# A Trainium2 kernel of a hybrid encoder: the first gate block of the attention branch moved to the end of the recurrence

## The chip, the cores and the metric

The kernel runs on one core of a Trainium2 chip. A core has TensorE (PE in the profile; its weight loads are PEld), VectorE (DVE), ScalarE (ACT), GpSimd (POOL) and SyncE (SP). Each takes its instructions in the order in which they are written, and they meet by semaphores alone. PE writes into eight PSUM banks (bank0 to bank7, each 128 x 512 fp32), from which VectorE and ScalarE read. The metric is the device time in microseconds of one execution of the whole program.

## The reference, cut to what matters

Two layers, each over x of 256 tokens x 2048 channels:

```python
for i in range(DEPTH):                       # 2
    proj = x @ w_in[i]
    y_a = s5_mixer(a_x, ...)                 # recurrence, gelu, then y * sigmoid(y @ w_glu + b_glu)
    y_a = y_a * silu(a_z)
    y_b = hyena_mixer(b_u, ...) * silu(b_z)  # short and long convolutions
    y_c = mla_mixer(c_q, c_kv, c_kr, ...) * silu(c_z)   # 8 heads of attention
    lifted = einsum('blnc,ncd->blnd', stack([y_a, y_b, y_c]), w_lift[i])
    gates = sigmoid(gate_logits)             # 3 x 2048 columns of proj
    mixed = sum(gates * lifted, axis=2) @ w_out[i]
    x = layer_norm(ALPHA * x + mixed + ple)
```

What the change moves is a piece of `gate_logits`: x times 512 columns of w_in, in the first of four column groups of the branch y_a. The code calls that stage "lifta", since the lifting of y_a goes with it; its 24 blocks are multiplied while the attention heads run, which is why the change is named after the attention branch.

## The kernel before

All weights lie in 184 blocks per layer, 128 x 2048 fp32 each, which SyncE streams in order into a ring of two blocks (four half slots). For most blocks ScalarE writes a rounded high part WH (`make_wh`, L380) and VectorE the rest WL = raw - WH (`make_wl`, L394; in the recurrence `make_wl_quarter`, L385), four quarters each. WH and WL hold one block: a quarter is written again when PE is done with it, and the slot of the ring is freed by the WL of its quarters. PE multiplies three products per tile: high x high, high x low, low x high.

A layer runs through the stages "ax" (8 blocks), "s5" (the recurrence, a loop of 8 turns with 8 blocks each), "glu" (4 blocks, not split, L1556), "mla" (queries, keys and values, 6 blocks, not split, L1556 and L1797, then the 8 heads), "lifta" within the heads, "hyc", "lift", "ple" and "out". Only the order of the code sets the order of the work. The table FILLS counts how often each bank is filled in each stage; the semaphores psum_full and psum_free of a bank count through the whole layer, so each wait is worked out from it.

At the end of the last turn of the recurrence PE multiplies `outputs` (L1724, L1729) into bank 7. VectorE adds (L834) and GpSimd sends the tile through y_scratch in HBM and back, and ScalarE makes the GELU of it (L1356), on which the gated unit waits. Before it PE multiplies the sums of squares of the latents (L1760) into banks 4 and 5; VectorE scales them (L841), ScalarE takes the roots (L1361), VectorE finishes (`inv_root`, L578 and on). The gated unit is 8 columns of 8 matmuls each (16 records each, for a full fp32 matmul has two) into banks 0 and 1 by turns, each read by a sigmoid on ScalarE (L1372), which must free the bank for the next column but one. The 12 columns of the queries and 8 of the keys use the same two banks (L1381, L1386), the values banks 2 and 3 (L1390).

The last block that is split in the recurrence's loop is already the first gate block, `lift_a(0)` = B_LIFT0. Its WH and WL are made at the end of the loop and stay as they are through the gated unit, queries, keys and values, until head 0 uses them. A block of a head is one call of `gated_block`: 4 quarters x 2 halves of the tokens x 3 products = 24 matmuls of 512 columns (L1599), into banks 0 and 1 for the four blocks of x, into banks 2 and 3 for the two of y_a. `attention(k)` is such a call for block k. Head h does: scores into banks 4 and 5 (L1820 to L1822), attention(3h), the transposes of the probabilities into bank 6 (L1830), attention(3h + 1), the product with the values into bank 7 (L1841), attention(3h + 2). VectorE does for head h: the maxima of the scores (L922), the normalising (L930), WL of block 3h + 1, a short convolution, the copy of bank 6 (L935), WL of block 3h + 2, a short convolution, the product from bank 7 (L942), WL of block 3h + 3, a short convolution. ScalarE does the exponentials (L1401) and then WH of the three blocks.

## Time and profile before

| | us |
|---|---|
| median of 3 runs | 2712.06 (2711.17 to 2716.62) |
| the profiled execution | 2707.26 |
| its span, first to last instruction | 2705.7 |
| PE busy in it | 2605.2 (96%) |
| VectorE busy | 1882.6 (70%) |
| ScalarE busy | 1275.7 (47%) |

The page gives the busy time of each engine and the mean clock that TensorE was granted (1.00 is 2.4 GHz, 0.50 is 1.2 GHz). The timeline lists instructions in order of time, those of one line merged: start, length, engine, line, operation, output and inputs, count, and in brackets the idle time of the engine just ahead and what ended it. The windows give busy times and the granted clock of a stretch. PE's matmuls overlap: one begins about 0.23 us after another while each is shown 0.39 us long, so lengths of a piece of work are read from start to start.

### The profile page before, as it was taken

Reading aid. Unit: us, or ns where it says so; the run is one execution under the profiler, and the core shown is the slowest. Engines: PE = TensorE matmul, PEld = TensorE weight load, DVE = VectorE, ACT = ScalarE, POOL = GpSimd, SP = SyncE. Lnnn points to the kernel's source line nnn. Section 1 sums busy time; section 2 is a strip of 40 time slices with the busy share of each in tenths; the row PEclk is TensorE's granted clock in tenths of the full one; section 3 lists DMA queues with packets and bytes.
Section 4 is the critical chain, followed back from the end, with each engine's and each line's share of the span. In section 5 each row is a group of like instructions: output and inputs, shape, how many; then the busy total and the mean of one; then the engine's idle time right before and its main releaser. Section 6 shows DMA issues by size and latency. Waiting matters only on the chain.

```text
span 2705.7 us, 41637 instructions
## 1 busy us (share of the span) xinstructions
PE 2605.2 (96%) x13736; PEld 2160.3 (80%) x13736; DVE 1882.6 (70%) x3315; ACT 1275.7 (47%) x2300; POOL 111.3 (4%) x206
## 2 busy tenths in 40 slices
PE   7999999999999999999989999999999999999998
PEld 6889998976776667898778999998777767678986
DVE  7788788735776767556678878776366767665666
ACT  5555555533443333443465555555344433244535
POOL 2100000000000000000020000000000000000000
PEclk9999999999999999999999999999999999999999
DMA  7544444434453324555464444443344524345554
GB/s 246 164 146 151 150 150 145 152 122 146 145 166 125 125 94 147 188 177 172 162 205 153 151 150 150 152 147 121 142 155 148 173 92 132 101 162 187 173 172 145
DMA packets 115956, 411.83 MB, mean 152 GB/s; under 512 B 15460, under 2 KB 15514, under 8 KB 115584
## 3 DMA queue, kind: packets, MB, share of 16 engines
q1 hardware_dynamic: 107424, 391.17, 43.8%
q0 software_dynamic: 8416, 19.18, 2.2%
q8 instruction: 66, 1.08, 0.2%
q14 instruction: 50, 0.41, 0.0%
HBM read 403.99 MB, written 6.29 MB: 152 GB/s over the span
## 4 chain that ended last, share of the span: by engine, by line
PE 90%; DVE 5%; issue 2%; ACT 2%; DMA 1%; PEldq 0%; PEld 0%; DVEq 0%; POOL 0%; POOLq 0%; ACTq 0%
PE bank L1599 28%; PE bank L1639 19%; PE bank L1641 10%; PE bank L1979 6%; PE bank L1556 5%; PE bank L1574 4%; PE bank L1729 2%; PE bank L1711 2%; PE bank L1692 2%; PE bank L1899 2%; PE bank L1797 1%; PE bank L1677 1%; PE bank L1879 1%; PE bank L1821 1%; PE bank L1913 1%
## 5 line engine op out<-in xcount | busy, mean ns | idle before, releaser
L380 ACT ACTIVATE WH<-ring 128x512 fp32r<-128x512 f32 x1364 | 854.5, 631 | 1204.4 <-PE bank L1599 541.1
L394 DVE TENSOR_TENSOR WL<-ring,WH 128x512 fp32r<-128x512 f32 x852 | 573.8, 689 | 455.5 <-ACT WH L380 453.4
L1639 PE MATMUL bank<-XX,WH 128*128 128x512 f32 x2304 | 820.8, 400 | 28.3 <-DVE XX L563 15.1
L1641 PE MATMUL bank<-XX,WL 128*128 128x256 f32 x2304 | 644.4, 280 | 0.0
L1639 PEld LDWEIGHTS bank<-XX,WH 128*128 128x128 f32 x2304 | 435.8, 189 | 129.3 <-issue 15.6
L1599 PE MATMUL bank<-WH,XX 128*128 128x512 f32 x1536 | 495.2, 404 | 11.7 <-DVE WL L394 8.3
L385 DVE TENSOR_TENSOR WL<-ring,WH 128x512 fp32r<-128x512 f32 x512 | 350.9, 688 | 137.1 <-ACT WH L380 133.2
L1641 PEld LDWEIGHTS bank<-XX,WL 128*128 128x128 f32 x2304 | 437.6, 190 | 0.0
L1599 PEld LDWEIGHTS bank<-WH,XX 128*128 128x128 f32 x1536 | 290.7, 192 | 91.5 <-issue 22.3
L1599 PE MATMUL bank<-WL,XX 128*128 128x512 f32 x768 | 304.9, 397 | 0.0
L1599 PEld LDWEIGHTS bank<-WL,XX 128*128 128x128 f32 x768 | 147.5, 192 | 32.2
L1556 PE MATMUL bank<-ARENA,ring 128*128 128x256 f32 x704 | 158.8, 388 | 13.6 <-ACT ARENA L1356 11.1
L1556 PEld LDWEIGHTS bank<-ARENA,ring 128*128 128x128 f32 x704 | 133.9, 194 | 37.9 <-issue 16.9
L1574 PE MATMUL bank<-XX,WH 128*128 128x256 f32 x640 | 115.9, 284 | 1.3 <-issue 1.3
L1979 PE MATMUL bank<-WL,MIXH 128*128 128x512 f32 x256 | 101.9, 398 | 0.0
L1574 PEld LDWEIGHTS bank<-XX,WH 128*128 128x128 f32 x640 | 99.7, 192 | 2.1 <-issue 2.1
L1979 PE MATMUL bank<-WH,MIXH 128*128 128x512 f32 x256 | 101.1, 395 | 0.0
L1979 PE MATMUL bank<-WH,MIXL 128*128 128x512 f32 x256 | 101.0, 395 | 0.0
L1574 PE MATMUL bank<-XX,WL 128*128 128x256 f32 x320 | 90.5, 283 | 0.0
L1729 PE MATMUL bank<-ARENA 128*128 128x64 f32 x512 | 67.6, 275 | 0.0
L1711 PE MATMUL bank<-ARENA 128*128 128x128 f32 x512 | 62.3, 275 | 0.0
L1729 PEld LDWEIGHTS bank<-ARENA 128*128 128x128 f32 x512 | 62.3, 192 | 0.0
(311 smaller groups left out, 3352.1 us busy)
## 6 DMA issues: line engine op xcount, KB each, us to landing
ring<-in_blocks SPq DMA_DIRECT2D x738, 512.0 KB, 3.4
ARENA<-in_bc POOLq DMA_DIRECT2D x2, 2048.0 KB, 8.3
ARENA<-in_decay POOLq DMA_DIRECT2D x8, 512.0 KB, 4.1
ARENA<-in_x SPq DMA_DIRECT2D x4, 512.0 KB, 8.3
u_scratch<-ARENA POOLq DMA_DIRECT2D x16, 128.0 KB, 2.4
ARENA<-u_scratch POOLq DMA_DIRECT2D x64, 32.0 KB, 3.1
y_scratch<-ARENA POOLq DMA_DIRECT2D x16, 128.0 KB, 2.0
ARENA<-y_scratch POOLq DMA_DIRECT2D x64, 32.0 KB, 2.7
```

Of the source, the lines that this page charges most:

```text
L380: nc.scalar.activation(wh[q], raw(which[0], q), ACT.Copy).then_inc(wh_ready[q], 1)
L385: nc.vector.tensor_tensor(wl[q], raw(which[0], q), wh[q].bitcast(F32), ALU.subtract).then_inc(w_used[slot(which[0], q // 2)], 1)
L394: vec.tensor_tensor(wl[q], raw(which[0], q), wh[q].bitcast(F32), ALU.subtract).then_inc(w_used[slot(which[0], half)], 1)
L1556: ins = mm(o, w[:, (w0 + i) * P:(w0 + i + 1) * P], rhs(i), start=i == 0, stop=i == k - 1)
L1574: ins = mm(o, w_, x_, start=start and i == 0 and n == 0, stop=stop and i == 7 and n == 2)
L1599: ins = mm(bank[b][:, :], x_, w_[q], start=first and n == 0, stop=last and n == 2)
L1639: ins = mm(bank[b][:, :], h, xx[:, :, k, :], start=(k == 0), stop=(k == DT - 1), skip_group_check=True)
L1641: ins = mm(bank[b][:, 0:T], l, xh[:, k, :], start=False, stop=(k == DT - 1), skip_group_check=True)
L1692: ins = mm(o, ET[:, q % 2 * CW + i * P:q % 2 * CW + (i + 1) * P], u4(q), start=True, stop=True)
L1711: ins = mm(bank[b][:, at:at + P], w_, f, start=(q % 2 == d == r == 0), stop=(q % 2 == d == r == 1), skip_group_check=True)
L1729: ins = mm(o, f, x_, start=False, stop=(d == 1 and r == 1))
L1979: ins = mm(bank[b][:, :], x_[:, k, token[t]], w_[q], start=False, stop=(k == 15 and n == 2), skip_group_check=True)
```

## The change

`attention(0)` is called once behind the loop of the recurrence, ahead of the sums of squares. It keeps banks 0 and 1 from there on, since the blocks 1 to 3 add to them. So the gated unit, the queries, the keys and the filter's two small matmuls use banks 2 and 3 where they used 0 and 1, and the values banks 6 and 7 where they used 2 and 3; the numbers in FILLS and in the waits follow. Head 0 now does: scores, attention(1), transposes, attention(2), product with the values. The other heads are as before. On VectorE, in head 0 alone, WL of block 3 is made ahead of the product from bank 7. ScalarE's order is unchanged.

```diff
@@ -97,10 +97,10 @@
 FILLS = {
     "ax":   [4, 4, 0, 0, 0, 0, 0, 0],
     "s5":   [32, 32, 8, 8, 24, 24, 0, 8],
-    "glu":  [4, 4, 0, 0, 0, 0, 0, 0],
-
-
-    "mla":  [11, 11, 2, 2, 9, 9, 8, 8],
+    "glu":  [0, 0, 4, 4, 0, 0, 0, 0],
+
+
+    "mla":  [0, 0, 11, 11, 9, 9, 10, 10],
...
@@ -931,20 +931,22 @@
                     make_wl(dve, v, layer, lift_a(3 * h + 1))
                     short_conv(3 * h)
-                    full(6, "mla", h)
+                    full(6, "mla", 2 + h)
                     free(v.tensor_copy(PT[:, (h % 2) * 2 * T:(h % 2 + 1) * 2 * T], bank[6][:, :]), 6)
                     make_wl(dve, v, layer, lift_a(3 * h + 2))
                     short_conv(3 * h + 1)
-                    full(7, "mla", h)
+                    if h == 0:
+                        make_wl(dve, v, layer, lift_a(3))
+                    full(7, "mla", 2 + h)
                     if h == 0:
                         dve.wait_ge(z_ready, layer * 3 + 3)
                     ins = v.tensor_tensor(tiles(YC, 0, 8)[:, h, :], bank[7][:, 0:T], PROJt[:, 50 + h, :], ALU.mult)
                     free(ins, 7)
-                    if h < HEADS - 1:
+                    if 0 < h < HEADS - 1:
                         make_wl(dve, v, layer, lift_a(3 * h + 3))
-                    else:
+                    elif h:
                         for half in range(2):
                             s_ = slot(B_W3, half)
                             dve.wait_ge(w_loaded[s_], load_number(layer, B_W3) * 16)
...
@@ -1368,26 +1370,26 @@
                 for m in range(WT):
                     if m == 6:
                         silu(0)
-                    full(m % 2, "glu", m // 2)
-                    ins = a.activation(SIG[:, m * T:(m + 1) * T], bank[m % 2][:, 0:T], ACT.Sigmoid, bias=par("b_glu", m))
-                    free(ins, m % 2)
+                    full(2 + m % 2, "glu", m // 2)
+                    ins = a.activation(SIG[:, m * T:(m + 1) * T], bank[2 + m % 2][:, 0:T], ACT.Sigmoid, bias=par("b_glu", m))
...
@@ -1753,6 +1755,10 @@
                     outputs()
+                attention = lambda k: gated_block("lifta", k // 6, k % 6, (xh, xl), (split(YAH, WT), split(YAL, WT)), lift_a(k))
+                attention(0)
+
+
                 for i in range(2):
                     pe.wait_ge(sq_ready, layer + 1)
                     take_bank(4 + i, "mla", 0)
@@ -1765,8 +1771,8 @@
                 pe.wait_ge(gelu_ready, layer + 1)
                 for m in range(WT):
                     w = unsplit(B_GLU + m // 2)
-                    take_bank(m % 2, "glu", m // 2)
-                    done(column(w, bank[m % 2][:, 0:T], lambda i: Ut[:, i, :], WT, w0=8 * (m % 2)), m % 2)
+                    take_bank(2 + m % 2, "glu", m // 2)
+                    done(column(w, bank[2 + m % 2][:, 0:T], lambda i: Ut[:, i, :], WT, w0=8 * (m % 2)), 2 + m % 2)
                     if m % 2:
                         used(B_GLU + m // 2)
...
@@ -1775,41 +1781,41 @@
                 pe.wait_ge(latent_ready, layer * 8 + 8)
                 for m in range(12):
                     w = unsplit(B_Q + m // 4)
-                    take_bank(m % 2, "mla", m // 2)
-                    done(column(w, bank[m % 2][:, 0:T], cq, LORA_T, w0=4 * (m % 4)), m % 2)
+                    take_bank(2 + m % 2, "mla", m // 2)
+                    done(column(w, bank[2 + m % 2][:, 0:T], cq, LORA_T, w0=4 * (m % 4)), 2 + m % 2)
                     if m % 4 == 3:
...
                 pe.wait_ge(late_loaded, layer * 64 + 48)
-                take_bank(0, "mla", 10)
-                done(mm(bank[0][:, 0:T], W1[0:33, :], FE[0:33, :], start=True, stop=True), 0)
+                take_bank(2, "mla", 10)
+                done(mm(bank[2][:, 0:T], W1[0:33, :], FE[0:33, :], start=True, stop=True), 2)
                 for half in range(2):
                     w = unsplit(B_V + half).rearrange("p (k c) -> p k c", k=4)
                     for t in range(2):
-                        take_bank(2 + t, "mla", half)
+                        take_bank(6 + t, "mla", half)
                         for i in range(LORA_T):
-                            ins = mm(bank[2 + t][:, :], ckv(i)[:, t * P:(t + 1) * P], w[:, i, :], start=(i == 0), stop=(i == LORA_T - 1))
+                            ins = mm(bank[6 + t][:, :], ckv(i)[:, t * P:(t + 1) * P], w[:, i, :], start=(i == 0), stop=(i == LORA_T - 1))
                             if i < LORA_T - 1:
                                 release(ins)
-                        done(ins, 2 + t)
+                        done(ins, 6 + t)
                     used(B_V + half)
...
@@ -1821,9 +1827,8 @@
                         release(mm(s, qt[r, h // 4, tok], kt[r, 0, :], start=False, stop=False))
                         done(mm(s, qt[r, 2 + h // 4, tok], kt[r, 1, :], start=False, stop=True), 4 + i)
-                    attention = lambda k: gated_block("lifta", k // 6, k % 6, (xh, xl), (split(YAH, WT), split(YAL, WT)), lift_a(k))
-                    attention(3 * h)
-                    take_bank(6, "mla", h)
+                    attention(3 * h if h else 1)
+                    take_bank(6, "mla", 2 + h)
                     for i in range(2):
                         pe.wait_ge(prob_ready, layer * 16 + (h * 2 + i + 1))
                         for kt_ in range(2):
@@ -1833,15 +1838,16 @@
                     if h == 1:
                         pe.wait_ge(yl_ready, layer * 3 + 1)
-                    attention(3 * h + 1)
-
-                    out_of(6, "mla", h)
-                    take_bank(7, "mla", h)
+                    attention(3 * h + 1 if h else 2)
+
+                    out_of(6, "mla", 2 + h)
+                    take_bank(7, "mla", 2 + h)
                     for k in range(2):
                         ins = mm(bank[7][:, 0:T], VV[:, k * W + h * P:k * W + (h + 1) * P],
                                  PT[:, (h % 2) * 2 * T + k * T:(h % 2) * 2 * T + (k + 1) * T], start=(k == 0), stop=(k == 1))
                     done(ins, 7)
-                    attention(3 * h + 2)
```

Behind the loop of the recurrence, PE. The rows are instructions in program order, with line, operation, output<-inputs, shape and count; L1724 and L1729 are the recurrence's outputs, L1760 the sums of squares, L1556 the gated unit. Before:

```order
L1729 MATMUL bank7<-ARENA_49 128x64 x4
L1662 REGISTER_ALU
L1662 COMPARE_AND_BRANCH
L1757 REGISTER_ALU
L1523 ISA
L1760 MATMUL bank4<-ARENA_49,CON 128x256 x4
L1760 MATMUL bank5<-ARENA_49,CON 128x256 x4
L1546 ISA
L1523 REGISTER_ALU
L1556 MATMUL bank0<-ARENA_49,ring 128x256 x8
L1556 MATMUL bank1<-ARENA_49,ring 128x256 x8
```

In the change (lines are two to six higher; L1601 is the gate block, of which the last six matmuls stand here, L1766 the sums, L1558 the gated unit):

```order
L1601 MATMUL bank0<-WH,XX 128x512 x2
L1601 MATMUL bank0<-WL,XX 128x512
L1601 MATMUL bank1<-WH,XX 128x512 x2
L1601 MATMUL bank1<-WL,XX 128x512
L1763 REGISTER_ALU
L1525 REGISTER_ALU
L1766 MATMUL bank4<-ARENA_49,CON 128x256 x4
L1766 MATMUL bank5<-ARENA_49,CON 128x256 x4
L1548 REGISTER_ALU
L1525 ISA
L1558 MATMUL bank2<-ARENA_49,ring 128x256 x8
L1558 MATMUL bank3<-ARENA_49,ring 128x256 x8
```

The whole gate block now stands between the recurrence and the sums of squares, and the gated unit fills banks 2 and 3.

The end of head 0, PE: L1841 is the product with the values, L1599 a gate block, L1820 to L1822 the scores. Before:

```order
L1526 REGISTER_ALU
L1523 ISA
L1841 MATMUL bank7<-ARENA_49 128x256 x2
L1599 MATMUL bank0<-WH,XX 128x512 x2
L1599 MATMUL bank0<-WL,XX 128x512
L1599 MATMUL bank1<-WH,XX 128x512 x2
L1599 MATMUL bank1<-WL,XX 128x512
```

In the change (L1846 is the product with the values, L1826 to L1828 the scores of head 1):

```order
L1601 MATMUL bank1<-WH,XX 128x512 x2
L1601 MATMUL bank1<-WL,XX 128x512
L1528 REGISTER_ALU
L1846 MATMUL bank7<-ARENA_49 128x256 x2
L1525 REGISTER_ALU
L1826 MATMUL bank4<-ARENA_49 128x256
L1827 MATMUL bank4<-ARENA_49 128x256
L1828 MATMUL bank4<-ARENA_49 128x256
L1826 MATMUL bank5<-ARENA_49 128x256
```

The third gate block of head 0 is gone: the scores of head 1 follow on the product with the values.

Head 0, VectorE: L935 copies bank 6, L394 makes WL of a block, L911 to L914 are a short convolution, L942 is the product from bank 7. Before:

```order
L935 COPY ARENA_49<-bank6 128x512
L393 REGISTER_ALU
L394 TENSOR_TENSOR WL<-ring,WH 128x512 x4
L911 TENSOR_SCALAR ARENA_49<-ARENA_49,PAR 128x256
L162 REGISTER_ALU
L912 SCALAR_TENSOR_TENSOR ARENA_49<-ARENA_49,PAR 128x255
L162 REGISTER_ALU
L914 SCALAR_TENSOR_TENSOR ARENA_49<-ARENA_49,PAR 128x255
L572 ISA
L942 TENSOR_TENSOR ARENA_49<-bank7,ARENA_49 128x256
L393 REGISTER_ALU
L394 TENSOR_TENSOR WL<-ring,WH 128x512 x4
```

In the change, from the WL of block 2 on (the rows ahead of it are as before, the copy of bank 6 still ahead of it; L944 is the product from bank 7):

```order
L394 TENSOR_TENSOR WL<-ring,WH 128x512 x4
L910 REGISTER_ALU
L911 TENSOR_SCALAR ARENA_49<-ARENA_49,PAR 128x256
L162 REGISTER_ALU
L912 SCALAR_TENSOR_TENSOR ARENA_49<-ARENA_49,PAR 128x255
L162 REGISTER_ALU
L914 SCALAR_TENSOR_TENSOR ARENA_49<-ARENA_49,PAR 128x255
L393 REGISTER_ALU
L394 TENSOR_TENSOR WL<-ring,WH 128x512 x4
L572 ISA
L944 TENSOR_TENSOR ARENA_49<-bank7,ARENA_49 128x256
```

The WL of block 3 moved ahead of the product from bank 7.

## Rows read from the trace of the kernel before

**Rows 1.** The page's busy times, and the span with its mean clock.

```profile
PE 2605.2 (96%) x13736; PEld 2160.3 (80%) x13736; DVE 1882.6 (70%) x3315; ACT 1275.7 (47%) x2300; POOL 111.3 (4%) x206
...
core 0: 2705.7 us, clock 0.985
```

**Rows 2.** Timeline of PE: start, us, line, operation, count [idle before, releaser].

```profile
537.37 3.67 PE L1760 MATMUL bank<-ARENA,CON 128*128 128x256 f32 x16
546.56 40.62 PE L1556 MATMUL bank<-ARENA,ring 128*128 128x256 f32 x176 [5.52 <-ACT ARENA L1356]
...
1885.68 8.97 PE L1556 MATMUL bank<-ARENA,ring 128*128 128x256 f32 x32 [5.56 <-ACT ARENA L1356]
1894.99 31.32 PE L1556 MATMUL bank<-ARENA,ring 128*128 128x256 f32 x144 [0.34 <-ACT ARENA L1372]
```

**Rows 3.** Windows: length, busy of PE, PEld, DVE, ACT, POOL, clock, DMA.

```profile
541.00:546.50 5.50, 0.04 (x1) 0.00 (x0) 0.00 (x0) 2.07 (x5) 2.20 (x4) 0.82 0.10 24
546.50:552.50 6.00, 5.94 (x17) 4.87 (x18) 4.34 (x8) 1.44 (x2) 0.00 (x0) 0.60 0.00 0
...
1885.70:1891.70 6.00, 6.00 (x20) 5.00 (x21) 4.43 (x8) 1.36 (x2) 0.00 (x0) 0.70 0.00 0
```

**Rows 4.** Timeline of PE, head 0 of layer one and head 1's start.

```profile
631.20 0.72 PE L1599 MATMUL bank<-WH,XX 128*128 128x512 f32 x2
...
636.79 0.60 PE L1830 MATMUL bank<-CON,ARENA 128*128 128x128 f32 x4
...
642.70 1.02 PE L1841 MATMUL bank<-ARENA 128*128 128x256 f32 x4
643.38 0.82 PE L1599 MATMUL bank<-WH,XX 128*128 128x512 f32 x2
...
649.06 0.59 PE L1820 MATMUL bank<-ARENA 128*128 128x256 f32 x2
```

**Rows 5.** Timelines of ScalarE (ACT) and VectorE (DVE), head 0 of layer one.

```profile
631.05 1.28 ACT L1401 ACT_TABLE_LOAD   x1
...
633.26 0.63 ACT L380 ACTIVATE WH<-ring 128x512 fp32r<-128x512 f32 x1
...
633.92 0.69 DVE L394 TENSOR_TENSOR WL<-ring,WH 128x512 fp32r<-128x512 f32 x1
...
639.63 0.69 DVE L935 COPY ARENA<-bank 128x512 f32<-128x512 f32 x1
640.23 1.31 DVE L394 TENSOR_TENSOR WL<-ring,WH 128x512 fp32r<-128x512 f32 x2
```

**Rows 6.** Timelines of ScalarE and VectorE at the seam, layer one.

```profile
553.52 0.42 ACT L1361 ACTIVATE ARENA<-ARENA 128x256 f32<-128x256 f32 x1 [5.57 <-DVE ARENA L841]
553.95 1.28 ACT L1372 ACT_TABLE_LOAD   x1
555.25 0.47 ACT L1372 ACTIVATE ARENA<-bank,PAR 128x256 f32<-128x256 f32 x1
...
534.60 0.41 DVE L693 TENSOR_TENSOR ARENA<-ARENA,bank 128x256 f32 x1
...
553.07 0.42 DVE L841 TENSOR_SCALAR ARENA<-bank 128x256 f32<-128x256 f32 x1
```

**Rows 7.** Timeline of PE: three other idle times, at stage changes.

```profile
72.39 0.49 PE L1639 MATMUL bank<-XX,WH 128*128 128x512 f32 x1 [2.22 <-DVE ARENA L591]
...
1413.20 0.49 PE L1639 MATMUL bank<-XX,WH 128*128 128x512 f32 x1 [2.21 <-DVE ARENA L591]
...
1041.71 0.74 PE L1599 MATMUL bank<-WH,XX 128*128 128x512 f32 x2 [2.73 <-DVE WL L394]
```

**Rows 8.** Windows of 6 us behind these three.

```profile
72.40:78.40 6.00, 6.00 (x25) 5.21 (x26) 2.51 (x5) 1.26 (x2) 2.91 (x6) 0.72 0.47 152
1413.20:1419.20 6.00, 6.00 (x35) 5.27 (x36) 4.08 (x8) 1.90 (x3) 2.91 (x6) 1.00 0.50 156
1041.70:1047.70 6.00, 4.77 (x13) 3.28 (x14) 6.00 (x8) 3.49 (x5) 1.09 (x2) 0.72 0.46 163
```

More of the change, by code:

```diff
@@ L851, in _ @@
                 for m in range(WT):
-                    out_of(m % 2, "glu", m // 2)
+                    out_of(2 + m % 2, "glu", m // 2)
                     st.did(v.tensor_tensor(SIG[:, m * T:(m + 1) * T], SIG[:, m * T:(m + 1) * T], PROJt[:, 34 + m, :], ALU.mult)); st.wait()
-                full(0, "glu", 3)
-                full(1, "glu", 3)
+                full(2, "glu", 3)
+                full(3, "glu", 3)
                 for m in range(WT):
@@ L890, in _ @@
                 for i in range(2):
-                    full(i, "mla", 10)
+                    full(2 + i, "mla", 10)
                     if i:
                         dve.wait_ge(hid_ready, layer * 2 + 1)
-                    free(v.tensor_scalar(ARG[0], bank[i][:, 0:T], par(f"b{i + 1}"), par(f"freq{i}"), ALU.add, ALU.mult), i)
-                    out_of(i, "mla", 10)
+                    free(v.tensor_scalar(ARG[0], bank[2 + i][:, 0:T], par(f"b{i + 1}"), par(f"freq{i}"), ALU.add, ALU.mult), 2 + i)
+                    out_of(2 + i, "mla", 10)
                     round_phase(dve, st, *ARG, arg_ready)
@@ L1378, in _ @@
                         silu(m // 4)
-                    full(m % 2, "mla", m // 2)
+                    full(2 + m % 2, "mla", m // 2)
                     dst = tiles(QN, 0, 8)[:, m, :] if m < 8 else tiles(QR, 0, 4)[:, m - 8, :]
-                    free(a.activation(dst, bank[m % 2][:, 0:T], ACT.Copy), m % 2)
+                    free(a.activation(dst, bank[2 + m % 2][:, 0:T], ACT.Copy), 2 + m % 2)
                 act.wait_ge(glu_done, layer * 8 + 8)
@@ L1384, in _ @@
                 for m in range(8):
-                    full(m % 2, "mla", 6 + m // 2)
-                    free(a.activation(tiles(KN, 0, 8)[:, m, :], bank[m % 2][:, 0:T], ACT.Copy), m % 2)
+                    full(2 + m % 2, "mla", 6 + m // 2)
+                    free(a.activation(tiles(KN, 0, 8)[:, m, :], bank[2 + m % 2][:, 0:T], ACT.Copy), 2 + m % 2)
                 for t in range(2):
                     for tok in range(2):
-                        full(2 + tok, "mla", t)
-                        free(a.activation(VV[:, tok * W + t * CW:tok * W + (t + 1) * CW], bank[2 + tok][:, :], ACT.Copy), 2 + tok)
+                        full(6 + tok, "mla", t)
+                        free(a.activation(VV[:, tok * W + t * CW:tok * W + (t + 1) * CW], bank[6 + tok][:, :], ACT.Copy), 6 + tok)
                     act.wait_ge(arg_ready, layer * 2 + (t + 1))
@@ L1398, in _ @@
                         if h:
-                            full(6, "mla", h - 1)
+                            full(6, "mla", 1 + h)
                         free(a.activation(PR[:, i * T:(i + 1) * T], bank[4 + i][:, 0:T], ACT.Exp, bias=SM[:, i * 4 + 1:i * 4 + 2],
@@ L1783, in _ @@
                     w = unsplit(B_K + m // 4)
-                    take_bank(m % 2, "mla", 6 + m // 2)
-                    done(column(w, bank[m % 2][:, 0:T], ckv, LORA_T, w0=4 * (m % 4)), m % 2)
+                    take_bank(2 + m % 2, "mla", 6 + m // 2)
+                    done(column(w, bank[2 + m % 2][:, 0:T], ckv, LORA_T, w0=4 * (m % 4)), 2 + m % 2)
                     if m % 4 == 3:
@@ L1794, in _ @@
                     for t in range(2):
[L1795 removed]
+                        take_bank(6 + t, "mla", half)
                         for i in range(LORA_T):
[L1797 removed]
+                            ins = mm(bank[6 + t][:, :], ckv(i)[:, t * P:(t + 1) * P], w[:, i, :], start=(i == 0), stop=(i == LORA_T - 1))
                             if i < LORA_T - 1:
                                 release(ins)
[L1800 removed]
+                        done(ins, 6 + t)
                     used(B_V + half)
                 pe.wait_ge(hid_ready, layer * 2 + 1)
[L1804 to L1805 removed]
+                take_bank(3, "mla", 10)
+                done(mm(bank[3][:, 0:T], W2[0:64, :], H1[0:64, :], start=True, stop=True), 3)
                 pe.wait_ge(qk_ready, layer * 2 + 2)
[L1808 removed]
+                for b in (2, 3):
                     out_of(b, "mla", 9)
[L1811 to L1812 removed]
+                out_of(6, "mla", 1)
+                out_of(7, "mla", 1)
                 qn, qt, kn, kt = tiles(QN, 0, 8), tiles(QT, 0, 4), tiles(KN, 0, 8), tiles(KT, 0, 4)
```

16 lines of the change are left out of this document (7 added, 9 removed).

## The prediction

> **What bounds the kernel now.** I read the page first: TensorE is busy 96% of the span at a mean granted clock of 0.985 [rows 1]. So time is won only where PE stands idle, runs at the low clock, or has work removed, and the change removes no matmul. The next view was PE's timeline at the seam between the recurrence and the gated unit. PE issues the sums of squares at 537.37, has their last record over at 541.04, and stands idle 5.52 us until the GELU, which waits for the y_scratch round trip; the second layer shows the same with 5.56 us [rows 2]. The third view was the windows behind that idle time: the clock has fallen inside it and stays low for the first part of the gated unit (mean 0.60 over 6 us in layer one, 0.70 in layer two, where 1.00 is the 2.4 GHz level and 0.50 the 1.2 GHz level) [rows 3]. Last came the timelines of head 0, the place that the block is taken from [rows 4, 5].
>
> **The block at the seam.** Block 0 is 24 matmuls, which PE gets through in 636.79 - 631.20 = 5.59 us [rows 4]. Its splits and banks are there: VectorE adds the last bank of the recurrence at 534.60, behind the four splits on its queue, before PE ends the recurrence at 537.37 [rows 2, 6]. So the block runs 537.37 to 542.96, and the sums of squares (3.5 us of issue, 3.67 with the last tail) end at 546.5. The GELU releases PE at 546.56, so the gated unit starts when it does now. The sums are read 5.6 us later; VectorE needs the first by 547.5 (the square root runs after the GELU on ScalarE) and the second by 553.07 [rows 6], so this costs nothing. **Front: 0.**
>
> **The clock of the gated unit.** PE is now busy up to 546.5 and has the full clock at once. At that clock a column (16 records) takes 31.32/144 x 16 = 3.48 us [rows 2], so two columns end at 546.56 + 6.96 = 553.5 instead of near 555.9. That would be 2.3 us won, but the third column needs the bank that Sigmoid 0 reads, and ScalarE starts that at 555.25, behind square root 1 (553.52, after VectorE's 553.07) and a table load of 1.28 us; none of these starts earlier [rows 6]. In layer two PE already waits 0.34 us for just this [rows 2]. The third column starts at about 555.9 as before: the gain turns into an idle time of 2.2 to 2.4 us. What that does to the clock is bounded by two rows of the trace: after 2.22 us idle at 72.39 the 6 us behind it have a mean clock of 0.72, after 2.21 us at 1413.20 they have 1.00 [rows 7, 8]. The fall costs 6 x 0.28 = 1.7 us; so each layer costs 0 to 1.7, and I take one of two. **Gated unit: 0 to +3.4, taken +1.7 in all.**
>
> The same ScalarE row bears on a rule of the Trainium skill ("ScalarE: Activation LUTs", What ACT_TABLE_LOAD costs): a switch of table takes about 1.28 us of load and about 1.38 us of drain. Here Sigmoid 0 starts 1.30 us after its load began, with no such drain seen [rows 6]. By the page's figure Sigmoid 0 would come 1.4 us later, the idle time would be an estimated 3.7 us, the clock would fall in both layers, and the sum would be 1.7 us higher.
>
> **Head 0 without block 0.** Today block 0 covers the softmax of head 0. In the change PE goes from the scores to block 1, whose splits both ScalarE and VectorE make after the softmax: table load at 631.05, two exponentials, first WH at 633.26, first WL at 633.92 + 0.69 = 634.61 [rows 5]. What is queued behind the scores' maxima on VectorE is thus what PE waits for. PE would have started at 631.20 [rows 4] and starts at about 634.7: a wait of 3.5 us. Later quarters are split in 0.63 and 0.69 us against 1.4 us of PE time, so they don't hold it. Block 1 then ends at 634.7 + 5.59 = 640.29 and the transposes follow until about 640.9. Now a second wait shows: VectorE copies the transposes out before it splits block 2. Today the copy comes at 639.63, long after the transposes of 636.79, and PE is inside block 1 [rows 4, 5]. In the change the copy starts at about 640.95, WL follows 0.60 later (640.23 - 639.63) and takes 0.69, so PE starts block 2 at 642.3, after 1.7 us idle. Block 2 ends at 647.9, the value product takes 643.38 - 642.70 = 0.68, and the scores of head 1 start at 648.55 instead of 649.06 [rows 4]. Taking out 5.6 us leaves 0.5, since 5.2 us of waits come up. **Head 0: -0.5 per layer, -1.0 in all.** The splits of block 3 now stand on VectorE before the product with bank 7. They are made while PE runs block 2, and PE needs them 3.3 us after head 0 ends, so this costs nothing.
>
> **The clock in head 0.** After 2.73 us idle at 1041.71 the 6 us behind it have 0.72 [rows 7, 8]; after 5.5 us idle they have 0.60 and 0.70 [rows 3]. An idle time of 3.5 us lies between. The price is 6 x 0.28 = 1.7 to 6 x 0.40 = 2.4 us; nothing hides it, as the transposes and the copy wait for PE. I take 1.8, nearer the 2.73 us row. **+3.6 in all, bounds 0 and +4.8** (0 since a 2.21 us idle time left the clock up). For the second idle piece, 1.7 us, I take nothing, and up to 1.7 us per layer as the upper bound.
>
> **The banks.** The gated unit, queries and keys move from banks 0 and 1 to 2 and 3, the values from 2 and 3 to 6 and 7. They are still pairs with one reader each, the recurrence frees 2, 3 and 6 before it ends, and bank 7 is taken by the values only behind the keys. DMA: blocks 0 and 1 keep their ring slots, whose release comes from the splits, which don't move. Both nothing. No step is moved past SP's or POOL's queues.
>
> **The sum.** 0 + 1.7 - 1.0 + 3.6 = +4.3 us. The profiled execution took 2707.26 us (span 2705.7 and 1.56 around it), so it would be 2711.6; the median of the runs shown is 4.8 us above it, which gives 2716.4.
>
> **Rivals.** (1) The clock is not lowered by the new idle times: -1.0, 2711.1. For it: 2.21 us at 1413.20 left it up [rows 7, 8]. Against: the clock fell at or behind 2.22, 2.73 and both times 5.5 us [rows 3, 7, 8], and head 0's is 3.5. (2) Slower: the clock falls behind each of the new idle pieces, the 2.3 us in the gated unit and the 1.7 us in head 0 as well, in both layers: 4 x 1.7 = 6.8 in place of the 1.7, so -1.0 + 3.6 + 6.8 = +9.4, 2721.5. It decides from the point at which an idle time near 2 us is enough; at 72.39 it was [rows 7]. (3) The block hides as it would if only the seam counted: the splits of block 1 are ready when the scores end. Then head 0 gives 5.6 less the 1.7 of the copy, 3.9 per layer and no clock fall: -7.8, 2704.3. Against it stands the order on both engines. (4) The change doesn't fill the seam: block 0 starts late, for a bank or a split, by up to its length. Of 5.6 us the later wait for Sigmoid 0 takes 2.3, so 3.3 per layer are left: 4.3 + 6.6 = +10.9, 2723. The rows at 534.60 speak against it [rows 6].
>
> **How the numbers follow.** Forecast 0.50 at 2716.4, with 2714 to 2719 as its own range (no or both falls in the gated unit); rival 1 0.16; rival 2 and cases between it and the forecast 0.22; rival 3 0.07; rival 4 0.05. 0.2%, about what a measurement of this kernel can tell from no change, is 5.4 us: 2706.6 to 2717.5. Faster: rival 3 and a tail, 0.08. Slower: rivals 2 and 4 and 0.12 of the forecast, where both layers fall in the gated unit, 0.39. Same: 0.53. The range runs from rival 1 with some scatter, 2708.5, to rival 2 with some, 2722.5, and leaves out rival 3, half of rival 4 and the tails, under 0.2.
>
> **What would show it.** In the profile after: PE without a gap from the recurrence to the gated unit; the gated unit's start about 9.2 us after the recurrence's last matmuls, as now; then an idle time of some 2.3 us before its third column, released by ScalarE; in head 0 an idle time of 3.5 us before block 1, released by VectorE's split, and one of 1.7 us before block 2; a clock of 0.5 at or behind the first of these. Wrong if block 1 starts right behind the scores, if the gated unit ends earlier than now, or if the clock stays at 1.00 through head 0.

## The result, and the profile of the kernel after

The changed kernel took 2716.73 us, the median of 12 runs (2712.96 to 2719.80), and the kernel before 2711.75 us beside it (12 runs, 2706.96 to 2717.35). The ratio is 1.0018 with a 95% interval of 1.0009 to 1.0026: about 5 us slower, just inside the 0.2% that this kernel's measurement can tell from no change. The forecast was 2716.4. The profiled execution took 2719.15 us.

The page of the kernel after, against [rows 1]: busy time of each engine, then the span and its mean clock.

```profile
PE 2612.2 (96%) x13736; PEld 2164.7 (80%) x13736; DVE 1881.3 (69%) x3315; ACT 1275.4 (47%) x2300; POOL 110.9 (4%) x206
...
core 0: 2717.6 us, clock 0.985
```

As many instructions on every engine as before, and PE 7 us more busy: matmuls that ran at the low clock count longer. Where that is, the timeline of PE tells. First the seam of layer one, against [rows 2]: start, us, line, operation, count [idle before, releaser].

```profile
543.53 3.61 PE L1766 MATMUL bank<-ARENA,CON 128*128 128x256 f32 x16
547.24 7.17 PE L1558 MATMUL bank<-ARENA,ring 128*128 128x256 f32 x32
556.54 31.32 PE L1558 MATMUL bank<-ARENA,ring 128*128 128x256 f32 x144 [2.13 <-ACT ARENA L1374]
...
1902.15 31.32 PE L1558 MATMUL bank<-ARENA,ring 128*128 128x256 f32 x144 [2.13 <-ACT ARENA L1374]
```

The block (L1601) starts at 537.96, the sums of squares (L1766) follow at 543.53, and the gated unit (L1558) at 547.24 without a gap: the idle time of 5.52 us is gone. Two columns now take 7.17 us, the speed of the full clock, where they took 8.97 in layer two [rows 2]. But the third column doesn't start earlier: PE waits 2.13 us for the first Sigmoid (L1374), in both layers. ScalarE's timeline says why, against [rows 6].

```profile
554.19 0.42 ACT L1363 ACTIVATE ARENA<-ARENA 128x256 f32<-128x256 f32 x1 [5.57 <-DVE ARENA L841]
554.62 1.28 ACT L1374 ACT_TABLE_LOAD   x1
555.92 0.84 ACT L1374 ACTIVATE ARENA<-bank,PAR 128x256 f32<-128x256 f32 x2
```

The second square root comes at 554.19, then the Sigmoid's table is loaded, and the Sigmoid starts at 555.92, 17.96 us behind the first work after the recurrence; before it was 555.25 - 537.37 = 17.88. ScalarE stood idle 5.57 us ahead of that second root, and VectorE's timeline shows for what:

```profile
548.65 1.75 DVE L578 RECIPROCAL ARENA<-ARENA 128x256 f32<-128x256 f32 x1 [2.78 <-ACT ARENA L1363]
...
553.74 0.42 DVE L841 TENSOR_SCALAR ARENA<-bank 128x256 f32<-128x256 f32 x1
```

PE was done with the second sum of squares by 547.24, but VectorE's scaling of it (L841) stands in the code behind the finishing of the first root and the scaling of the first latents (L578 to L847). So what holds the third column begins with VectorE's order. No run moves that line. Now head 0 of layer one, against [rows 4]. The scores (L1826 to L1828) end ahead of the first row; L1601 is a block, L1835 the transposes, L1846 the value product.

```profile
635.15 1.22 PE L1601 MATMUL bank<-WH,XX 128*128 128x512 f32 x2 [3.49 <-DVE WL L394]
...
643.32 0.60 PE L1835 MATMUL bank<-CON,ARENA 128*128 128x128 f32 x4
645.30 0.73 PE L1601 MATMUL bank<-WH,XX 128*128 128x512 f32 x2 [1.38 <-DVE WL L394]
...
650.88 1.03 PE L1846 MATMUL bank<-ARENA 128*128 128x256 f32 x4
651.74 0.59 PE L1826 MATMUL bank<-ARENA 128*128 128x256 f32 x2
```

And VectorE there, against [rows 5].

```profile
634.40 2.50 DVE L394 TENSOR_TENSOR WL<-ring,WH 128x512 fp32r<-128x512 f32 x4
...
643.95 0.69 DVE L935 COPY ARENA<-bank 128x512 f32<-128x512 f32 x1 [5.69 <-PE bank L1835]
644.56 2.49 DVE L394 TENSOR_TENSOR WL<-ring,WH 128x512 fp32r<-128x512 f32 x4
```

Block 1 waits 3.49 us for its first split (634.40), which stands on VectorE behind the maxima and reciprocals of the softmax. Block 2 waits 1.38 us, since VectorE copies the transposes out (643.95) before it splits block 2 (644.56). Layer two has the same two waits, 3.48 at 1980.82 and 1.38 at 1990.60. The windows of the two stretches show the clock: busy of PE, PEld, DVE, ACT, POOL, then the granted clock and DMA.

```profile
556.50:562.50 6.00, 5.96 (x28) 5.29 (x29) 3.17 (x8) 0.73 (x2) 0.00 (x0) 1.00 0.46 175
...
632.00:634.00 2.00, 0.00 (x0) 0.00 (x0) 1.18 (x7) 1.99 (x6) 1.01 (x2) 0.98 0.55 220
634.00:636.00 2.00, 0.85 (x2) 0.76 (x3) 1.96 (x5) 1.93 (x4) 0.00 (x0) 0.50 0.01 1
636.00:638.00 2.00, 2.00 (x6) 1.54 (x6) 1.93 (x5) 0.00 (x0) 0.00 (x0) 0.50 0.56 170
638.00:640.00 2.00, 2.00 (x6) 1.55 (x5) 0.27 (x1) 0.63 (x1) 0.00 (x0) 0.50 0.76 252
```

Behind the gated unit's 2.13 us the clock stays at 1.00. In head 0 it falls within the wait, which begins at 635.15 - 3.49 = 631.66: it is 0.98 up to 634 and 0.50 from there on. Block 1 runs at 0.50, the 1.2 GHz level, and its 24 matmuls take 643.32 - 635.15 = 8.17 us in place of 5.59 [rows 4].

So I measured each kernel between two of its own points, which leaves the scatter of the rest of the program out: from the first work behind the recurrence to the first score of head 1. Before this is 111.69 us in layer one and 111.84 in layer two; after, 651.74 - 537.96 = 113.78 and 1997.04 - 1883.66 = 113.38. The change costs 2.09 + 1.54 = 3.6 us there. The profiled spans differ by 11.9 us; the other 8.3 lie in code whose order the change doesn't touch, 4.5 of them between head 1 of layer one and the end of layer two's recurrence. At the start of that recurrence the same GpSimd gathers behind a round trip through u_scratch waited 2.13 us in one execution and 5.60 in the other, and PE stood idle there in the second only. GpSimd's timeline of before (the first row) and of after, and PE's of after:

```profile
1424.29 2.43 POOL L447 DMA_DIRECT2D ARENA<-u_scratch  x4 [2.13 <-DMA u_scratch<-ARENA]
```

```profile
1435.04 2.43 POOL L447 DMA_DIRECT2D ARENA<-u_scratch  x4 [5.60 <-DMA u_scratch<-ARENA]
```

```profile
1440.17 0.50 PE L1641 MATMUL bank<-XX,WH 128*128 128x512 f32 x1 [2.00 <-DVE ARENA L693]
```

A second profile of the unchanged after (below, "after_again") had a span of 2713.3 us, of which only 1.3 us more than before lie outside the stretch. The profile of banks_only (below), which moves no block, has the stretch of before and a span of 2712.3 us, 6.6 more. So I take the 8.3 us for scatter and no part of the change's price.

### The profile page after: what moved, and what is told of

Same layout as the page of the kernel before. It is cut to its first block, busy times and chain, and to the rows that moved or that the text cites. A ratio compares the mean times of both kernels' runs of the same rounds, so it can differ in the third digit from the quotient of the medians.

```text
span 2717.6 us, 41717 instructions
## 1 busy us (share of the span) xinstructions
PE 2612.2 (96%) x13736; PEld 2164.7 (80%) x13736; DVE 1881.3 (69%) x3315; ACT 1275.4 (47%) x2300; POOL 110.9 (4%) x206
## 4 chain that ended last, share of the span: by engine, by line
PE 87%; DVE 6%; issue 3%; ACT 2%; DMA 2%; PEldq 0%; DVEq 0%; POOL 0%; PEld 0%; POOLq 0%; ACTq 0%
PE bank L1601 28%; PE bank L1641 18%; PE bank L1643 9%; PE bank L1985 6%; PE bank L1558 5%; PE bank L1576 4%; PE bank L1731 2%; PE bank L1713 2%; PE bank L1694 2%; PE bank L1905 2%; PE bank L1803 1%; PE bank L1885 1%; PE bank L1679 1%; DMA u_scratch<-ARENA 1%; PE bank L1919 1%
## 5 line engine op out<-in xcount | busy, mean ns | idle before, releaser
L394 DVE TENSOR_TENSOR WL<-ring,WH 128x512 fp32r<-128x512 f32 x852 | 572.5, 688 | 452.0 <-ACT WH L380 450.0
L1601 PE MATMUL bank<-WH,XX 128*128 128x512 f32 x1536 | 499.7, 407 | 22.4 <-DVE WL L394 19.1
L1601 PEld LDWEIGHTS bank<-WH,XX 128*128 128x128 f32 x1536 | 294.0, 194 | 103.7 <-DVE WL L394 22.3
L1601 PE MATMUL bank<-WL,XX 128*128 128x512 f32 x768 | 307.1, 400 | 0.0
L1601 PEld LDWEIGHTS bank<-WL,XX 128*128 128x128 f32 x768 | 148.8, 194 | 32.6
L1558 PE MATMUL bank<-ARENA,ring 128*128 128x256 f32 x704 | 154.9, 381 | 6.4 <-ACT ARENA L1374 4.3
L1558 PEld LDWEIGHTS bank<-ARENA,ring 128*128 128x128 f32 x704 | 131.5, 190 | 29.2 <-issue 8.1
```

What stands on the lines that cost most here:

```text
L394: vec.tensor_tensor(wl[q], raw(which[0], q), wh[q].bitcast(F32), ALU.subtract).then_inc(w_used[slot(which[0], half)], 1)
L1558: ins = mm(o, w[:, (w0 + i) * P:(w0 + i + 1) * P], rhs(i), start=i == 0, stop=i == k - 1)
L1601: ins = mm(bank[b][:, :], x_, w_[q], start=first and n == 0, stop=last and n == 2)
```

## The experiments

The theory: the banks and the seam cost nothing, the gated unit keeps its length and may lose the clock behind its new wait, and head 0 loses a little by waits less than it won by the moved block, plus the clock behind the wait of 3.5 us. The rivals: the banks cost something; the clock is not the price, the waits are; or the split of block 3, made earlier on VectorE, delays PE. Each diff is against the kernel after unless it says otherwise. "The stretch" is the one just defined, in layer one / layer two.

### The banks alone

Block 0 goes back behind the scores of head 0, and VectorE's order there too; the banks stay changed.

```
-                attention(0)
...
-                    attention(3 * h if h else 1)
+                    attention(3 * h)
...
-                    attention(3 * h + 1 if h else 2)
+                    attention(3 * h + 1)
...
-                    if h:
-                        attention(3 * h + 2)
+                    attention(3 * h + 2)
```

> The change's banks and counts alone: gated unit, queries and keys in banks 2 and 3, values in 6 and 7, block 0 back in head 0. Theory (the cost is made in head 0 and by the clock): no difference from the kernel before, ratio 1.000, PE idle 5.5 us ahead of the gated unit, no wait ahead of a block in head 0. Rival (the other banks cost something, by a later release or by sharing with readers): a ratio near the 1.0018 of the whole change.

Measured: 0.9992 (0.9983 to 1.0001), median 2708.27 us. The stretch is 111.71 / 111.74 us against 111.69 / 111.84, the idle time at the seam is back with 5.58 and 5.57 us, and PE waits for no split in head 0. The waits of PE in layer one, line and releaser: us, times, longest.

```profile
PE bank L1556 <- ACT ARENA L1356: 5.6, 1, 5.6
PE bank L1556 <- ACT ARENA L1381: 0.5, 1, 0.5
PE bank L1556 <- ACT ARENA L1372: 0.3, 1, 0.3
```

The new banks are free, and what the change costs comes from moving the block.

### The wait filled with other matmuls

Fourteen surplus matmuls, whose result nobody reads, stand between the scores and block 1 of head 0. They fill PE's idle time; the split that block 1 waits for comes when it did.

```
+                    if h == 0:
+                        for n in range(14):
+                            mm(bank[7][:, :], xh[:, 0, token[0]], xx[:, :, 0, :], start=True, stop=True, ...)
                     attention(3 * h if h else 1)
```

> The changed kernel with 14 surplus matmuls of 512 columns (about 3.1 us at the full clock) into bank 7 in head 0, between the scores and block 1; their results are never read. VectorE's and ScalarE's work is untouched, so the wait for the first WL stays where it is. Theory (idle time lowers the clock, and the lower clock costs 2.6 and 2.2 us in block 1): the clock stays at 1.00 in head 0, block 1 takes 5.6 us instead of 8.2 and 7.8, ratio to before 1.0018 - 4.8/2712 = 1.0000. Rival (block 1 is slow as its splits come late): block 1 stays at about 8 us and the ratio at 1.0018.

Measured: 1.0010 (1.0000 to 1.0021), median 2713.03 us. The timeline of PE: the surplus matmuls (L1832), block 1's first quarter right behind them.

```profile
630.57 3.47 PE L1832 MATMUL bank<-XX 128*128 128x512 f32 x14
634.14 0.74 PE L1601 MATMUL bank<-WH,XX 128*128 128x512 f32 x2
```

The window over them and block 1:

```profile
631.00:641.00 10.00, 9.25 (x42) 7.08 (x40) 5.95 (x15) 6.43 (x13) 1.01 (x2) 1.00 0.42 148
```

Block 1 starts 97.14 us behind the first work after the recurrence, against 97.19 in after: it is no earlier. It takes 5.62 us instead of 8.17, and head 0 (first score to first score of head 1) takes 20.99 / 20.90 us, where after has 23.49 / 23.11 and before 21.20 / 21.20. This separates the two: the fallen clock costs 2.5 and 2.2 us per layer, and the waits, less the moved block, win 0.2 and 0.3. The timing moved less than these 4.7 us: 3.7 by the medians, and 2.2 by the ratios, each taken to the kernel before beside it. In part that may be the gated unit: in this profile the clock fell behind its 2.13 us in layer two, which put the last matmul ahead of the scores (the filter's second small one) 1.9 us later.

### The splits of block 1 made early

ScalarE makes the high parts of block 1 behind the last value copy, and VectorE the low parts before it reads the last filter phase, so both are done before the scores.

```
+                    if t:
+                        for half in range(2):
+                            make_wh(act, half, layer, lift_a(1))
...
                 for i in range(2):
+                    if i:
+                        make_wl(dve, v, layer, lift_a(1))
                     full(2 + i, "mla", 10)
...
-                    make_wl(dve, v, layer, lift_a(3 * h + 1))
+                    if h:
+                        make_wl(dve, v, layer, lift_a(3 * h + 1))
                     short_conv(3 * h)
...
-                        for half in range(2):
+                        for half in range(2) if h or b else ():
                             make_wh(act, half, layer, lift_a(3 * h + 1 + b))
```

> The changed kernel with the high part of block 1 made on ScalarE behind the last read of the values, and its low part on VectorE ahead of the filter's second phase, instead of behind the softmax of head 0. Theory: PE goes from the scores into block 1 without a wait, 3.5 us and the clock's 2.4 us per layer are gone, 11.8 us in all, ratio 1.0018 - 0.0044 = 0.9974; the wait ahead of block 2 stays at 1.4 us. Rival (the softmax, now later, holds the transposes): the wait comes back ahead of the transposes and the ratio is 1.000 or above.

Measured: 0.9988 (0.9979 to 0.9997), median 2708.53 us. The stretch is 109.92 / 110.15 us, 3.9 and 3.2 less than after. Block 1 runs right behind the scores, and what is late next is block 2. PE, then VectorE:

```profile
636.83 0.60 PE L1841 MATMUL bank<-CON,ARENA 128*128 128x128 f32 x4
639.52 1.20 PE L1607 MATMUL bank<-WH,XX 128*128 128x512 f32 x2 [2.10 <-DVE WL L394]
```

```profile
636.82 0.41 DVE L913 TENSOR_SCALAR ARENA<-ARENA,PAR 128x256 f32<-128x256 f32 x1
...
638.19 0.68 DVE L938 COPY ARENA<-bank 128x512 f32<-128x512 f32 x1
638.79 2.49 DVE L394 TENSOR_TENSOR WL<-ring,WH 128x512 fp32r<-128x512 f32 x4
```

Softmax, short convolution (L913), copy, split: VectorE does them in this order, and the wait ahead of block 2 grows from 1.38 to 2.10 us. The first quarter of block 2 takes 1.20 us for what 0.73 does at the full clock. So the clock fell here too, with a wait of 2.10 us, and block 2 took 7.2 us in place of 5.6. Of the 11.8 us expected, 7.1 came.

### The split of block 2 ahead of the copy

In head 0 VectorE makes the low parts of block 2 before it copies the transposes out.

```
+                    if h == 0:
+                        make_wl(dve, v, layer, lift_a(2))
                     full(6, "mla", 2 + h)
                     free(v.tensor_copy(PT[...], bank[6][:, :]), 6)
-                    make_wl(dve, v, layer, lift_a(3 * h + 2))
+                    if h:
+                        make_wl(dve, v, layer, lift_a(3 * h + 2))
```

> The changed kernel with VectorE, in head 0, splitting block 2 ahead of the copy of the transposes. Theory: the second wait of 1.38 us per layer is gone, PE goes from the transposes into block 2, and nothing comes up later, since the copy is needed 5.5 us later: 2.8 us, ratio 1.0008; the 3.5 us wait and the low clock ahead of it stay. Rival (the second wait is hidden by something else in head 1): the wait goes but the time stays at 1.0018.

Measured: 1.0010 (1.0001 to 1.0019), median 2713.73 us. PE's timeline in head 0 of layer one:

```profile
635.11 1.22 PE L1604 MATMUL bank<-WH,XX 128*128 128x512 f32 x2 [3.50 <-DVE WL L394]
...
643.44 0.60 PE L1838 MATMUL bank<-CON,ARENA 128*128 128x128 f32 x4
643.79 0.70 PE L1604 MATMUL bank<-WH,XX 128*128 128x512 f32 x2
```

The second wait is gone and the first is as it was. Head 0 takes 22.02 / 21.90 us, 1.5 and 1.2 less than after. The stretch is 113.98 / 113.79 all the same, because the clock fell in the gated unit of both layers this time (the last matmul ahead of the scores 1.7 and 1.6 us later). A window there, at the low level:

```profile
556.00:557.00 1.00, 1.00 (x3) 0.73 (x3) 0.96 (x3) 0.00 (x0) 0.00 (x0) 0.50 0.25 70
```

### Four banks for the gated unit

The gated unit's columns go round four banks, so that the third column needs no bank that Sigmoid 0 has to read.

```
-    "glu":  [0, 0, 4, 4, 0, 0, 0, 0],
+    "glu":  [0, 0, 2, 2, 0, 0, 2, 2],
...
-                    full(2 + m % 2, "glu", m // 2)
+                    full(GLU_BANKS[m % 4], "glu", m // 4)
```

with GLU_BANKS = (2, 3, 6, 7), and the same on PE and VectorE.

> The changed kernel with the gated unit's eight columns going round four banks (2, 3, 6, 7) instead of two. Theory (the third column waits for the bank of Sigmoid 0, which ScalarE can't start earlier): the wait of 2.13 us per layer goes, PE runs through four columns, ratio 1.0018 - 4.3/2712 = 1.0002. Rival (ScalarE's later work, its SiLU and table loads, is the bound of this stretch): the wait comes back as idle time at the queries, and the ratio stays at 1.0018.

Measured: 0.9976 (0.9967 to 0.9985), median 2706.00 us. PE's timeline:

```profile
547.46 38.25 PE L1559 MATMUL bank<-ARENA,ring 128*128 128x256 f32 x176
```

The wait of 2.13 us is gone: eleven columns in one piece. The last matmul ahead of the scores comes 87.02 / 87.31 us behind the first work after the recurrence, 2.3 and 2.0 less than after. Head 0 has its two waits and its low clock as in after (22.75 / 22.88 us), and the stretch is 110.75 / 111.13. That is 3.0 and 2.3 less, in all 5.3, while the median says 10.7 less than after. So I timed it a second time beside the kernel after on one chip:

> The changed kernel with four banks for the gated unit once more, beside the changed kernel on the same chip. Its profile accounts for 5.3 us between recurrence and head 1, the first timing gave 11. If the rest is scatter (the clock's falls elsewhere come at other places from run to run), it is 5 to 7 us below the changed kernel here, ratio 0.9995 to 1.000. If four banks bring something that the profile of that stretch doesn't show, it is 10 us or more below, ratio under 0.998 again.

> The changed kernel itself, as the other one's neighbour: ratio 1.0018, within 1.0009 to 1.0026. The wait of 2.1 us ahead of the third column of the gated unit lowers the clock in about half of the layers (4 of 10 in the profiles so far), the wait of 3.5 us in head 0 in all.

Measured: glu4 1.0010 (0.9999 to 1.0021), median 2713.26 us; the kernel after 1.0025 (1.0016 to 1.0034), median 2716.42. Side by side four banks win 0.0015, about 4 us, with intervals that overlap; the profiles of the second time say 110.46 / 110.47 for glu4 and 114.10 / 115.78 for after, 9.0 us in all. The first 0.9976 doesn't stand: two timings of one kernel lie 0.34% apart, so an interval from one timing of this kernel is too narrow to read single terms from, and the readings here go by the stretch in the profiles, term by term. The second profile of after also shows what the first didn't: in layer two the clock fell behind the gated unit's wait (the last matmul ahead of the scores at +91.27 instead of +89.33), and the change cost 2.4 + 3.9 = 6.3 us in the two stretches.

### Four banks in the kernel before

The same edit on the kernel before, with banks 0 to 3.

> The kernel before with the gated unit's columns going round banks 0 to 3. Here PE starts the gated unit at the low clock. Theory (the low clock's 2.3 us are hidden today behind the wait for Sigmoid 0, and only the block at the seam uncovers them): no wait for the bank is left to remove but layer two's 0.34 us, ratio 1.000. Rival (two banks hold the gated unit in any case): as large a gain as in the changed kernel with four banks.

Measured: 0.9994 (0.9985 to 1.0003), median 2710.06 us. In layer one the stretch is 111.71 us, as before: behind the 5.6 us of idle time the columns run at the low clock and the third is hardly held. Without the block at the seam there is nothing to win. In layer two the stretch was 115.60 us, 3.8 more than before. Of these, 3.2 came from a place that nobody expected, the scores of head 0. PE's timeline:

```profile
1972.60 0.67 PE L1821 MATMUL bank<-ARENA 128*128 128x256 f32 x2 [0.35 <-ACT ARENA L1391]
...
1975.57 1.06 PE L1823 MATMUL bank<-ARENA 32*128 32x256 f32 x2
1976.56 1.22 PE L1600 MATMUL bank<-WH,XX 128*128 128x512 f32 x2
```

and the windows:

```profile
1969.00:1975.00 6.00, 5.65 (x18) 2.50 (x17) 2.41 (x6) 0.60 (x1) 0.00 (x0) 1.00 0.23 84
1975.00:1976.00 1.00, 1.00 (x4) 0.78 (x4) 0.82 (x3) 0.65 (x2) 0.00 (x0) 0.63 1.02 401
...
1977.00:1982.00 5.00, 5.00 (x13) 3.85 (x13) 1.87 (x7) 1.70 (x6) 0.66 (x2) 0.50 0.06 18
```

The clock fell inside the scores, where PE had not stood idle for more than 0.35 us, and head 0 took 24.38 us instead of 21.20.

### The split of block 3 back behind the product

VectorE's order for block 3 as it was before the change.

> The changed kernel without its reordering on VectorE: in head 0 the low part of block 3 is made behind the product from bank 7, as in the other heads. Theory (block 3 is needed 3.3 us after head 0 ends, so its order costs nothing): ratio 1.0018. Rival (behind the product it comes too late for head 1, or the maxima of head 1 do): a wait ahead of block 3 of up to 1 us per layer, ratio 1.0025.

Measured: 1.0023 (1.0014 to 1.0032), median 2717.79 us. The waits of PE in layer one:

```profile
PE bank L1599 <- DVE WL L394: 4.9, 2, 3.5
PE bank L1556 <- ACT ARENA L1372: 2.1, 1, 2.1
```

They are those of after, and the stretch is 113.70 / 115.73, the second with the clock fallen in the gated unit. Block 3 belongs to head 1, behind the stretch: from its first score to that of head 2 it is 21.35 us in before, after and this run, in both layers. The reordering on VectorE costs nothing, and this rival falls.

### All three repairs

The early splits of block 1, the split of block 2 ahead of the copy, and the four banks, in one kernel.

> The changed kernel with the early split of block 1, the late copy and the four banks together. Theory: the gains add up to 11.8 + 2.8 + 4.3 = 18.9 us against the changed kernel, ratio to before 1.0018 - 0.0070 = 0.9948, PE without an idle time over 0.5 us from the recurrence to the end of the heads. Rival (they share a bound, ScalarE's or VectorE's queue): less than two thirds of that, ratio above 0.997.

Measured: 0.9945 (0.9931 to 0.9958), median 2696.72 us (5 runs). PE, in head 0:

```profile
633.98 0.60 PE L1845 MATMUL bank<-CON,ARENA 128*128 128x128 f32 x4
636.02 0.74 PE L1611 MATMUL bank<-WH,XX 128*128 128x512 f32 x2 [1.45 <-DVE WL L395]
```

The stretch is 105.35 / 105.57 us, 8.4 and 7.8 less than after, and the clock stays up. One wait is left, 1.45 and 1.50 us ahead of block 2, now for the short convolution that VectorE does between the softmax and the split. So one more kernel puts the split of block 2 ahead of it, too (the diff is against all3):

```
-                    if h:
-                        make_wl(dve, v, layer, lift_a(3 * h + 1))
+                    make_wl(dve, v, layer, lift_a(3 * h + 1 if h else 2))
                     short_conv(3 * h)
-                    if h == 0:
-                        make_wl(dve, v, layer, lift_a(2))
```

> The three alterations together, and in head 0 the low part of block 2 made ahead of the first short convolution as well. In the run before it PE still waited 1.45 us ahead of block 2, while VectorE did the convolution (1.36 us) in front of that split. Theory (this wait is the convolution): it shrinks to some 0.1 to 0.3 us, 2.4 us in both layers, ratio 0.9945 - 0.0009 = 0.9936. Rival (the wait is the softmax, which ends just ahead of the convolution, or ScalarE's high part of block 2): it stays above 1 us, ratio 0.9945.

Measured: 0.9948 (0.9936 to 0.9961), median 2697.14 us (6 runs). PE's timeline and the windows of layer two:

```profile
634.57 0.72 PE L1608 MATMUL bank<-WH,XX 128*128 128x512 f32 x2 [0.20 <-DVE WL L395]
```

```profile
1957.00:1963.00 6.00, 5.75 (x18) 2.77 (x17) 2.47 (x5) 2.67 (x5) 0.00 (x0) 1.00 0.24 90
1963.00:1964.00 1.00, 1.00 (x4) 0.58 (x4) 0.93 (x4) 0.00 (x0) 0.00 (x0) 0.72 0.98 393
1964.00:1966.00 2.00, 2.00 (x6) 1.52 (x6) 1.71 (x5) 0.12 (x1) 0.00 (x0) 0.50 0.97 297
```

The wait went from 1.45 to 0.20 us, and head 0 of layer one from 17.47 to 16.18. In layer two it went only to 17.26: the clock fell late in the scores and stayed low for some 3 us, much as in before_glu4. The stretch is 104.39 / 105.21 us. The profile puts all4 1.3 us ahead of all3, of 2.4 expected, and the timing can't tell them apart. By the ratios, taken on two chips, both are 14 to 15 us below the kernel before and beat the change by 0.7%; the two stretches of all3 give 12.6 us of that.

## Why the prediction was right, point by point

**The front, forecast 0.** Right. The gated unit starts 9.28 and 9.19 us behind the first work after the recurrence, before 9.19 and 9.24.

**The gated unit, forecast an idle time of 2.2 to 2.4 us and +1.7 for one clock fall in two layers.** The wait is 2.13 us, for Sigmoid 0, and glu4 shows the cause, as it goes when the third column has a bank of its own. Of the fall the profiled after has none: from the first work behind the recurrence to the first score it is 0.2 and 0.4 us shorter than before. Over the six profiles that have this wait (after twice, fill_wait, early_split, copy_late, wl3_late) the clock fell in 5 of 12 layers, at 1.6 to 1.9 us each, read at the last matmul ahead of the scores. That is 0.8 falls in two layers, so the choice of one in two was near, and the bounds of none and both were both seen. The Trainium skill ("ScalarE: Activation LUTs", What ACT_TABLE_LOAD costs) adds a drain of some 1.38 us to the load. Again it doesn't show: the Sigmoid starts 1.30 us after its load began, and the wait is 2.13 us, not the estimated 3.7.

**Head 0 without block 0, forecast -1.0.** Measured -0.5 at the full clock (fill_wait: 20.99 and 20.90 against 21.20). The places are right: 3.5 us in idle time ahead of block 1 (3.49), and the copy ahead of block 2, which from the start of the transposes to the block took 645.30 - 643.32 = 1.98 us where I had worked out 642.3 - 640.29 = 2.0. What was mis-sized is small: the value product takes 651.74 - 650.88 = 0.86 us ahead of scores, not 0.68 as ahead of a block, and block 1 needs 5.62 and not 5.59.

**The clock in head 0, forecast +3.6 from the 2.73 us row.** The mechanism was right and the size too low: 2.5 and 2.2, together +4.7 us, at the upper bound of 4.8. Here the clock stood at 0.50 from 634 to 640 us, where the 6 us behind the 2.73 us had a mean of 0.72 [rows 8]; the nearer row would have been the windows behind 5.5 us [rows 3], at 2.4 us. It fell in every one of the 12 layers with a wait of 3.5 us and nothing to fill it (after twice, copy_late, glu4 twice, wl3_late). How much that costs varies: block 1 took from 7.05 us (glu4_again) to 8.43 us (wl3_late) where the full clock takes 5.6, so 1.5 to 2.8 us per layer, and in the second profile of after 2.7 in both, above the forecast's bound of 2.4.

**The banks and VectorE's order, forecast 0.** Right, by banks_only and wl3_late.

**The sum.** +4.3 forecast. In the two profiles of after, +3.6 (no fall in the gated unit) and +6.3 (one fall); in the medians +5.0 and, the second time, +6.9. In the first profile errors offset each other: the clock in head 0 cost 1.1 more, its waits 0.5 more, and the gated unit with what follows up to the scores 2.3 less. The mechanisms are those forecast. That the median came out within 0.4 us of the forecast is luck: terms were off by up to 2.3 us, and 4 us can hardly be told from nothing here.

**The rivals.** (1), no fall, is out by the windows of head 0. (2), a fall behind each idle piece, happened in part: in the gated unit in 5 of 12 layers; behind the 1.38 us ahead of block 2 the block ran at the full clock (its first quarter 0.73 us). early_split shows that piece with 2.10 us, and there the clock fell in both layers, in the second some 0.9 us into block 2. (3), block 1 ready in time, was not so in the kernel, and early_split made it so: of the 3.9 us per layer that the rival gave against before, 1.8 and 1.7 came, since the wait ahead of block 2 grew to 2.10 us and took the clock along. I had not followed what the copy and the short convolution do to block 2 when block 1 comes earlier. (4) is out: the seam is filled.

Open is what decides whether 2.13 us of idle time lowers the clock; the same wait at the same place gave both. Open is also why the clock fell inside the scores three times.

## What to carry to other kernels

A block of work moved from one gap to another pays only if the cover it leaves is not needed: read, at the place it leaves, which engine would be late, for how long, and count the clock behind that wait as a term of its own (here 2.2 to 2.5 us in head 0, while the waits, less the moved block, cost nothing). A filled gap gives nothing back while the next stage still waits for the same slow chain; here the gain of the seam turned into a wait of 2.13 us until the columns had more banks. The repairs in head 0 were not on PE: splits made earlier on ScalarE and VectorE, and a copy moved behind a split on VectorE.

## What the runs showed of the hardware that was not expected

The granted clock fell to the 1.2 GHz level while PE was at work, with no idle time over 0.35 us ahead of it: in before_glu4 at 1975 (3.2 us lost) and in all4 at 1963 (1.1 us lost), each in head 0 of layer two, late in the scores, two thirds of whose matmuls have only 32 rows. In layer two of glu4_again it fell there as well, before the wait of 3.45 us had begun. PE's last score ends at 1966.23, and the windows of that run show:

```profile
1965.90:1966.00 0.10, 0.10 (x2) 0.00 (x0) 0.10 (x1) 0.10 (x1) 0.00 (x0) 1.00 0.99 410
...
1966.10:1966.20 0.10, 0.10 (x1) 0.00 (x0) 0.10 (x2) 0.10 (x1) 0.00 (x0) 0.50 1.19 492
```

So a fall that is counted with the 3.5 us wait need not come from the wait alone; whether the scores ahead of it have a share, no run tests. The Trainium skill ("TensorE: Matmul & The Clock Gate", Why this matters for your kernels) names idle gaps between bursts as what to avoid. By the rows here that alone doesn't keep the clock, but three falls in three profiles don't show what does.

Behind one and the same wait of 2.13 us in the gated unit the clock fell in 5 of 12 layers, behind the 2.10 us ahead of block 2 in early_split in 2 of 2, in or just ahead of the 3.5 us in 12 of 12, behind the 1.4 to 1.5 us ahead of block 2 in none of 14 (seven profiles, first quarter 0.72 to 0.74 us), and fourteen surplus matmuls in the place of the 3.5 us kept it at 1.00. So filler work can win time without making anything earlier: head 0 was 2.2 and 2.5 us shorter with it.
